# Two-layer trunk kernel: four sums per layer of the down projection's weights stored to DRAM and loaded again

## The reference

```python
for l in range(2):                                   # S = 512 rows, D = 1024, FFN_HIDDEN = 2816
    h = rms_norm(x, pre_mix_g[l]); z = h @ w_in[l]
    y_a = gmlp_mixer(gelu(u), gelu(v), ...)          # spatial gating, 4 groups
    y_b = diff_attention(q, k, v, ...)               # 4 heads, block-causal
    x = x + rms_norm(concat(y_a, y_b) @ w_out[l], post_mix_g[l])
    h = rms_norm(x, pre_ffn_g[l])
    gate, up = split(h @ w_gate_up[l])
    y = (silu(gate) * up) @ w_down[l]                # the stage of this case: 512x2816 times 2816x1024
    x = x + rms_norm(y, post_ffn_g[l])
```

## Time and profile before

| | |
|---|---|
| device time, 3 runs | 1069.54 us median (1069.37 to 1069.75) |
| the profiled execution | 1071.2 us, its span 1069.4 us |
| PE busy | 1058.6 us (99%), granted clock 0.998 |
| PE weight loads busy | 948.2 us |
| DVE, ACT, POOL busy | 789.2, 632.6, 499.0 us |
| DMA | 130.39 MB, mean 122 GB/s |
| raw loads of `w_down` | 54 of 512 KB (4.3 us median to landing), 14 of 256 KB (2.7 us) |
| `x_rows` from `x_spill` | 8 of 512 KB, 5.6 us median |

### The profile page before, as it was taken

One profiled execution on the slowest core, in us unless ns is written; L12 is line 12 of the kernel. 1 busy time (PEld: TensorE's weight loads), 2 busy tenths in 40 slices (PEclk: granted clock), 3 DMA queues, 4 the chain that ended last, 5 costly groups with the idle time before them and its releaser, 6 DMA issues.

```text
span 1069.4 us, 17811 instructions
## 1 busy us (share of the span) xinstructions
PE 1058.6 (99%) x6704; PEld 948.2 (89%) x6704; DVE 789.2 (74%) x1277; ACT 632.6 (59%) x1253; POOL 499.0 (47%) x378
## 2 busy tenths in 40 slices
PE   8999999999999999999999999999999999999997
PEld 7888888999999999888778888889999999998876
DVE  5376644878888886998754756548888888869996
ACT  6767684756555554644657578747555555545352
POOL 4535264457666665030444344634666666630310
PEclk9999999999999999999999999999999999999999
DMA  8423213424334333467353222133343433325662
GB/s 303 141 59 99 70 51 98 158 76 123 92 107 118 90 110 119 150 230 237 123 152 124 79 80 79 60 95 123 100 115 103 118 90 110 118 84 193 219 204 78
DMA packets 151161, 130.39 MB, mean 122 GB/s; under 512 B 4250, under 2 KB 120484, under 8 KB 151076
## 3 DMA queue, kind: packets, MB, share of 16 engines
q1 hardware_dynamic: 151060, 129.25, 38.5%
q10 hardware_dynamic: 16, 0.00, 0.0%
HBM read 122.95 MB, written 6.29 MB: 121 GB/s over the span
## 4 chain that ended last, share of the span: by engine, by line
PE 88%; DVE 7%; DMA 2%; ACT 2%; issue 1%; DVEq 0%; SPq 0%; ACTq 0%
PE banks L720 27%; PE banks L722 27%; PE banks L721 27%; PE banks L789 2%; PE banks L817 2%; DMA raw<-in_w_down_dram 2%; DVE w_lo L2184 2%; PE banks L729 1%; PE banks L802 1%; PE banks L1042 1%; PE banks L828 1%; ACT junk L1263 0%; DVE part_full L2148 0%; DMA x_rows<-in_x_dram 0%; DVE raw L2171 0%
## 5 line engine op out<-in xcount | busy, mean ns | idle before, releaser
L675 POOL TENSOR_TENSOR w_lo<-raw,w_hi 128x512 fp32r<-128x512 f32 x200 | 261.4, 1317 | 146.0 <-ACT w_hi L1338 141.5
L657 POOL TENSOR_TENSOR w_lo<-raw,w_hi 128x512 fp32r<-128x512 f32 x136 | 188.5, 1410 | 294.0 <-ACT w_hi L1255 293.9
L720 PE MATMUL banks<-xg_hi,w_hi 128*128 128x256 f32 (+1 forms) x880 | 273.5, 311 | 0.0
L722 PE MATMUL banks<-xg_lo,w_hi 128*128 128x256 f32 (+1 forms) x880 | 271.3, 308 | 0.0
L721 PE MATMUL banks<-xg_hi,w_lo 128*128 128x256 f32 (+1 forms) x880 | 271.2, 308 | 0.0
L1338 ACT ACTIVATE w_hi<-raw 128x512 fp32r<-128x512 f32 x200 | 124.6, 631 | 116.6 <-DVE raw L2078 62.4
L722 PEld LDWEIGHTS banks<-xg_lo,w_hi 128*128 128x128 f32 x880 | 168.0, 191 | 8.5
L720 PEld LDWEIGHTS banks<-xg_hi,w_hi 128*128 128x128 f32 x880 | 168.1, 191 | 8.3
L721 PEld LDWEIGHTS banks<-xg_hi,w_lo 128*128 128x128 f32 x880 | 168.1, 191 | 7.5
L721 PE MATMUL banks<-s_part,w_lo 128*128 128x256 f32 x480 | 135.8, 283 | 0.0
L720 PE MATMUL banks<-s_part,w_hi 128*128 128x256 f32 x480 | 135.8, 283 | 0.0
(11 more groups left out here) (231 smaller groups left out, 2190.2 us busy)
## 6 DMA issues: line engine op xcount, KB each, us to landing
raw<-in_w_gate_up_dram SPq DMA_DIRECT2D x88, 512.0 KB, 4.2
raw<-in_w_down_dram SPq DMA_DIRECT2D x54, 512.0 KB, 4.3
raw<-in_w_in_dram SPq DMA_DIRECT2D x40, 512.0 KB, 3.8
raw<-in_w_out_dram SPq DMA_DIRECT2D x16, 512.0 KB, 3.4
x_spill<-x_rows SPq DMA_DIRECT2D x8, 512.0 KB, 4.9
x_rows<-x_spill SPq DMA_DIRECT2D x8, 512.0 KB, 5.6
raw<-in_w_down_dram SPq DMA_DIRECT2D x14, 256.0 KB, 2.7
x_rows<-in_x_dram SPq DMA_DIRECT2D x4, 512.0 KB, 7.3
```

Source lines behind the costliest of these rows:

```text
L657: last = tt(lo[:, piece], raw_half(l, c, h)[:, piece], hi[:, piece].bitcast(F32), ALU.subtract)
L675: tt(lo, full, hi.bitcast(F32), ALU.subtract).then_inc(w_ready, 1)
L720: mm(o, stat[0], mov[0], start=first, stop=False)
L722: return mm(o, stat[0], mov[1], start=False, stop=last)
```

## The change

**T2 kept.** For P0 to P3 of each layer, T2 (which `pair_sums` forms anyway) stays in half 1 and is stored to DRAM (`t2_spill`, 256 KB each); T4 is formed in place of B21, by one DVE sum that moves from `pair_sums` into `pair_lows`, ahead of T3's low part. Half 0 of such a P is now loaded again after T4's low part, half 1 after T3's low part and the landed store. Q0 to Q3 load T2 (256 KB) and B22 (256 KB) where B11 (256 KB) and B12 over B22 (512 KB) were loaded, and form T1 = B22 - T2 by one sum.

**x rows.** Row blocks 2 and 3 are reloaded behind the layer's last weight loads, with a semaphore of their own, and so is the next layer's gain `gpre`; `gpost` goes ahead of row block 0.

**Boundary.** After layer 0, ACT's `xg_high(group, 1)` moves ahead of row 2's branch root, and DVE's `xg_low(group, 1)` between the first and second operation of `residual(b, 2)`.

```diff
+    N_KEPT = 4
+        t2_spill = nc.dram_tensor("t2_spill", [L, N_KEPT, P, SE], F32)
...
         def pair_raw(l, c, i):
-            row, col = ((0, 0), (1, 0), (0, 1), (1, 1))[i] if kind == "P" else ((0, 1), (0, 0), (1, 1))[i]
+            row, col = ((0, 0), (1, 0), (0, 1), (1, 0) if t2_kept(c) else (1, 1))[i] if kind == "P" else ((0, 1), (0, 0), (1, 1))[i]
...
         def load_half
-                    if kind_of(d) == "P":
+                    if kind_of(d) == "P" and t2_kept(d):
+                        sp.wait_ge(pair_ready, pair_upto(m, d, P_T3 if h else P_T4))
+                        if h == 1:
+                            sp.wait_ge(t2_stored, 16 * (N_KEPT * m + DOWN[d - C_DOWN][1] + 1))
+                    elif kind_of(d) == "P":
                         sp.wait_ge(pair_ready, pair_upto(m, d, P_T4 if h else P_B21))
...
+            def store_t2(l, c):
+                sp.wait_ge(pair_added, pair_added_upto(l, c, 1))
+                sp.dma_start(t2_spill[l, DOWN[c - C_DOWN][1]], raw_half(l, c, 1)[:, SE:2 * SE]).then_inc(t2_stored, 16)
             def load(l, c):
+                n = raw_n(l, c)
+                if n >= 2:
+                    m, d = RAW_ORDER[n - 2]
+                    if kind_of(d) == "P" and t2_kept(d):
+                        store_t2(m, d)
                 for h in range(2):
                     load_half(l, c, h)
...
-                    for r, behind in enumerate((C_L_END, C_Q[1], C_Q[3], C_Q[5])):
+                    for r, behind in enumerate((C_L_END, C_Q[1])):
...
+                if l < L - 1:
+                    load_gain(gpre[:, :], pre_mix_g[l + 1], gpre_landed)
+                for r in range(2, ST):
+                    sp.dma_start(x_rows[:, r, :], x_spill[r * P:(r + 1) * P, :]).then_inc(x_back_late, 16)
...
         ACT boundary
+                    if r == 2 and b % 2:
+                        xg_high(group, 1)
                     root_of_branch(b, l, r)
-                    if r == 2:
+                    if r == 2 and b % 2 == 0:
                         xg_high(group, 1)
...
         DVE boundary (residual calls between() behind tt(y_b, y_b, silu_t))
-                    residual(b, r)
-                    if r == 2:
+                    if r == 2 and b % 2:
+                        residual(b, r, lambda: xg_low(group, 1))
+                    else:
+                        residual(b, r)
+                    if r == 2 and b % 2 == 0:
                         xg_low(group, 1)
...
         pair_sums
-                        dve.wait_ge(pair_added, pair_added_upto(l, c, 1))
-                        tt(b22, b21, b22, ALU.subtract).then_inc(pair_added, 1)
+                        if not t2_kept(c):
+                            dve.wait_ge(pair_added, pair_added_upto(l, c, 1))
+                            tt(b22, b21, b22, ALU.subtract).then_inc(pair_added, 1)
+                    elif t2_kept(c):
+                        tt(b12, b22, b11, ALU.subtract).then_inc(pair_added, 1)
...
         pair_lows
+                        if kind_of(c) == "P" and t2_kept(c) and i == P_T3:
+                            b21, t2 = [raw_half(l, c, col)[:, SE:2 * SE] for col in range(2)]
+                            dve.wait_ge(pair_added, pair_added_upto(l, c, 1))
+                            tt(b21, b21, t2, ALU.subtract).then_inc(pair_added, 1)
```

More of the change, by code:

```diff
@@ L381, in pair_added_upto, with t2_kept @@
             kind, p = DOWN[c - C_DOWN]
-            return 5 * NP * l + (3 * p + i + 1 if kind == "P" else 3 * NP + 2 * p + i + 1)
+            per_layer = 5 * NP - N_KEPT
+            if kind == "P":
+                return per_layer * l + 3 * p + i + 1
+            return per_layer * l + 3 * NP + 2 * p - min(p, N_KEPT) + i + 1
+        def t2_kept(c):
+            return DOWN[c - C_DOWN][1] < N_KEPT
         def pair_upto(l, c, i):
@@ L531, in weights_of @@
             kind, n = DOWN[c - C_DOWN]
+            if kind == "Q" and n < N_KEPT:
+                if h == 0:
+                    return lambda t: t[:, 0:SE], t2_spill[l, n]
+                return lambda t: t[:, SE:2 * SE], w_dn_v[l, :, 2 * n + 1, HALF:D]
             if kind == "Q" and h == 0:
@@ L553, in load_half @@
                         sp.wait_ge(w_ready, low_upto(m, d, LOW_OF[B22 if h else T4] if blocks(d) else h))
+                if kind_of(c) == "Q" and t2_kept(c) and h == 0:
+                    sp.wait_ge(t2_stored, 16 * (N_KEPT * l + DOWN[c - C_DOWN][1] + 1))
                 view, src = weights_of(l, c, h)
                 sp.dma_start(view(raw_half(l, c, h)), src).then_inc(raw_landed[n % 2][h], 16)
+            def store_t2(l, c):
+                sp.wait_ge(pair_added, pair_added_upto(l, c, 1))
+                sp.dma_start(t2_spill[l, DOWN[c - C_DOWN][1]], raw_half(l, c, 1)[:, SE:2 * SE]).then_inc(t2_stored, 16)
             def load(l, c):
+                n = raw_n(l, c)
[3 more added lines that the diff above has]
+                        store_t2(m, d)
                 for h in range(2):
@@ L1628, in pair_high @@
                     kind, p = DOWN[c - C_DOWN]
-                    if (kind, i) in (("P", P_B11), ("P", P_B21), ("Q", Q_B22)):
+                    loaded = {("P", P_B11): 0, ("P", P_B21): 0, ("Q", Q_B22): 1}
+                    if t2_kept(c):
+                        loaded["Q", Q_T2] = 0
+                    if (kind, i) in loaded:
                         n = raw_n(l, c)
-                        act.wait_ge(raw_landed[n % 2][kind == "Q"], 16 * (n // 2 + 1))
+                        act.wait_ge(raw_landed[n % 2][loaded[kind, i]], 16 * (n // 2 + 1))
+                    elif kind == "P":
+                        act.wait_ge(pair_added, pair_added_upto(l, c, {P_T3: 0, P_T4: 2}[i]))
                     else:
-                        act.wait_ge(pair_added, pair_added_upto(l, c, {P_T3: 0, P_T4: 2}[i] if kind == "P" else i))
+                        act.wait_ge(pair_added, pair_added_upto(l, c, 0 if t2_kept(c) else i))
                     if ring[l, c, i][1] is not None:
@@ L1797, in add_eps, with residual @@
                 ts(bias_a[:, at], ssq_a[:, at], 1.0 / D, EPS, ALU.mult, ALU.add).then_inc(bias_a_ready, 1)
-            def residual(b, r):
+            def residual(b, r, between=lambda: None):
                 y_b = y_right_of(b, r)
@@ L1807, in residual @@
                     tt(y_b, y_b, silu_t[:, r, :], ALU.add).then_inc(y_b_added, 1)
+                    between()
                     if r == 0:
@@ L1819, in residual @@
                 if b % 2 and r == 0:
-                    dve.wait_ge(x_back, 16 * ST * (b // 2 + 1))
+                    dve.wait_ge(x_back, 32 * (b // 2 + 1))
+                elif b % 2 and r == 2:
+                    dve.wait_ge(x_back_late, 32 * (b // 2 + 1))
                 if b % 2:
```

8 lines of the change are left out of this document (4 added, 4 removed).

## The result

| | before | after |
|---|---|---|
| device time, median of 9 runs each | 1069.68 us (1068.67 to 1070.81) | 1071.44 us (1071.09 to 1072.88) |
| the profiled execution, its span | 1071.2, 1069.4 us | 1071.13, 1069.3 us |

The ratio is 1.0020 (1.0011 to 1.0029): 1.8 us slower, where 1067.5 us and a gain of 2 us were forecast.

What follows compares the result with a forecast made beforehand. PE, busy 99% of the span, was taken as the bound, with 3.7 us of stalls to win. Layer 0's 1.1 us and layer 1's 0.95 us made 2.05 us: 1069.5 to 1067.5 us, range 1066.2 to 1070.4 us.

Steps and rivals of the forecast that it cites:

- layer 0's 1.1 us: Layer 0's gain, limited by POOL's lows at the boundary: 1.2 us and not 2.6 us, taken as 1.1 us.
- 0.4 us at Q5 of layer 1: With x row block 3's load moved, Q5's 0.48 us stall in layer 1 goes but for some 0.1 us.
- The left halves: P0 to P3: T4's later sum adds 0.3 us of waits in all, costs PE nothing; thinnest cover 0.8 us.
- signs of being wrong: PE waits before P4 or P5, a store landing after 4 us, Q6's stall unchanged, or no POOL wait at the boundary.
- P0's 0.5 us: P0 ends about 0.5 us later, since T4's sum no longer fills DVE's wait for ACT ahead of `h_low`.
- The third rival: Late release of kept pairs' buffers makes PE wait at P4, P5 and P6: 1073.1 us; chance 0.09.
- P5 loses nothing: Layer 1's P5 had waited 1.56 us for a load and starts near 985.7 again, PE at 989.7.
- The right halves: Q0 to Q3: a 0.69 us sum saved each, counting only at Q0 and Q1; Q2's 0.47 us stall goes.
- The x rows: Moving x loads brings Q6's sums 1.8 us earlier in layer 0; 0.77 us at Q6, 0.6 us at R14 and R18 go.
- put down to the run: The profiled 1071.2 us stood 1.7 us above the median, ascribed to the run; 2.05 us was subtracted from 1069.5 us.
- The boundary: After layer 0, the 0.85 us at row block 1's product goes; POOL's lows then bind with about 1 us wait.
- The first rival: Boundary is free if ACT reaches the second chunk's highs early enough; layer 0 gives 2.5 us: 1065.9 us; chance 0.10.

Runs made afterwards that it cites:

- e3_t2: Kernel before plus only the T2 part, x row blocks and boundary as before: 1071.91 us, +2.2 us, ratio 1.0021 against before.
- e4_no_t2: The whole change without T2 kept (N_KEPT = 0), so moved loads and boundary order only: 1069.92 us, ratio 1.0000 against the kernel before.
- e9_sum_order: Kernel before plus only T4's later sum and the release that follows from it, nothing stored, Q as before: 1075.44 us, ratio 1.0053 against before.
- e10_sum_order_act: e9_sum_order with ACT's two large left-operand highs moved behind P4's and P5's: 1072.48 us, ratio 1.0024 against the kernel before.
- e6_late_release: Kernel before with only half 0 of P0 to P3's raw buffers released at the pair's end: 1069.99 us, ratio 0.9997 against before.
- e14_no_store: The whole change without its eight stores and the waits for them: 1071.71 us, ratio 1.0022 against the kernel before.
- e5_act_order: The whole change with ACT's two large left-operand highs moved behind P4's and P5's: 1070.26 us, ratio 1.0006 against the kernel before.
- e2_boundary: Kernel before plus only the change's order at the boundary: 1070.06 us, ratio 0.9999 against the kernel before.
- e7_early_highs: e4_no_t2 with ACT's two highs of the next layer's second chunk moved around row block 2's root: 1067.70 us, ratio 0.9980 against before.
- e0_before_again: The kernel before, run and profiled once more, unchanged: 1070.11 us, ratio 1.0004.

## Why the prediction was wrong, step by step

Of the 3.9 us between the forecast and the measured time, about 2.7 us lie in T2's part, which was to give some 0.5 us and costs 2.2 us (e3_t2). The rest is most of the gain of 1.5 us forecast for the moved loads and the boundary (layer 0's 1.1 us and 0.4 us at Q5 of layer 1), of which e4_no_t2 shows nothing (1.0000, 0.9992 to 1.0009).

- **The left halves ("this part costs PE nothing").** This is the step that failed and turned the sign. It counted "ACT's 0.63 us for its high part", "under 0.1 us of wait per pair", and looked for danger in the buffers. It never asked what stands behind T4's high on ACT: in P2, two highs of 1.69 us and then P3's. The waits per pair were right (0.09 to 0.10 us). Two of its own signs of being wrong came: PE waits before P5, and a store lands later than 4 us. Gross, the part costs 5.3 us (e9_sum_order), 3.0 us of it ACT's queue (e10_sum_order_act).
- **P0's 0.5 us** were right (0.45 us), and taken as harmless. Together with P4's or P5's data they put DVE's sum behind the start of POOL's lows in layer 0, 1.1 us more; that term was missing (last section).
- **The late release and the store.** The third rival had PE wait at P4, P5 and P6; it waits at P5 of layer 1 alone. "P5 loses nothing" took P3's end as unmoved. P3 ended 1.7 us later (980.87 for 979.15), P5's load went out behind it, and DVE began P5 at 987.17 where "near 985.7 again" was forecast. Alone the late release is free (e6_late_release), and in the change the stores are too (e14_no_store), but the latter because P3 is late. With P3 on time, its store holds back half 1 of P5's load, stores and loads in each other's way as the rival has it, and 0.45 us of the 0.72 us remain (e5_act_order). That the stores cost the change nothing is luck. The Trainium skill's warning (DMA: Bandwidth & Descriptors, section Anatomy of one DMA — SWDGE (gpsimd) path) that a write to HBM can confirm late fits the landing of the change's eight stores after issue,

```profile
DMA to landing us min/median/max: 2.0/2.5/5.0
```

against 2.0 us for the output's. Two took longer than the 4 us I allowed, P3's of both layers (4.8 and 5.0 us). In every run with stores P3's took 4.3 to 5.2 us, and P0's 2.0 us. P3's are issued about 1 us behind the second of P4's two loads, P0's with no weight load in flight; whether the loads or the write itself delays P3's, no run shows. The Trainium skill's fit there, by which 256 KB would take 2.6 us (an estimate), is given for DMAs that GpSimd issues; these are issued by SP.

- **The right halves.** That the sum saved in Q2 is swallowed by ACT's high was right. That little counts of Q0's and Q1's was right for DVE's slack of before and wrong for the delayed DVE: the shorter Qs pay back 3.1 us of the part's own 5.3 us. In layer 1 the sums of Q0 and Q1 gave 1.4 us back as counted, but DVE was 1.7 us late behind P6 (996.11 for 994.38), so it came to Q2 0.3 us later than before (1018.12 for 1017.83) and not 0.9 us earlier. That is why 0.32 us of the stall remain.
- **The x rows.** Mechanism right (0.30 us of wait for 1.49 us), size not: 0.6 us with an interval from 1.8 us to nothing. The 1.7 us by which the profiled execution stood above the median I "put down to the run", and then subtracted stalls of that same run from the median, so that a part of the gain was counted twice. The second profile of the kernel before stood above its median as well, with the same stalls in layer 0. That the runs at the median lack some of them was argued from the profiles of e2_boundary and e6_late_release, and no profile of a median execution of the kernel before shows it.
- **The boundary.** Right: POOL's lows bind, a wait of 1.00 us where about 1 us was named. But alone it is worth nothing (e2_boundary), since it trades one wait for the other. The first rival's condition, ACT's highs early enough, is what e7_early_highs makes true: 2.2 us against e4_no_t2, of which its profiles place 1.2 us at the boundary.

With these the account of the measured time closes, roughly: T2 +2.2 us (e3_t2) and the other parts between -0.6 and +0.2 us, against +1.8 us measured.

## What to carry to other kernels

When an operation moves later by less than a microsecond, list what is queued behind its consumer on every engine, not only what it feeds; a large instruction there carries the delay into the next item. Subtract a stall from a median only if it is in the median's executions: take a second profile, or compare the profiled time with the runs first. Once a part's cost and gain are measured apart (5.3 and 3.1 us here), a small net change shows where to mend; moving two ACT instructions was worth more than any part of the change. A part that a test shows to be free is free in that order only: the stores cost nothing while another delay covers them, and showed once it was mended.

## What the runs showed of the hardware

One DVE sum of 128x1024 takes nearly twice as long when POOL is first. Layer 1 of the profile of before, and of the same kernel in e0_before_again:

```profile
993.80 9.32 POOL L657 TENSOR_TENSOR w_lo<-raw,w_hi 128x512 fp32r<-128x512 f32 x4 [42.49 <-ACT w_hi L1255]
994.38 2.31 DVE L2157 TENSOR_TENSOR hid_full<-hid_hi,part_full 128x1024 f32<-128x1024 f32 x1
```
```profile
992.87 1.22 DVE L2157 TENSOR_TENSOR hid_full<-hid_hi,part_full 128x1024 f32<-128x1024 f32 x1
...
993.69 9.05 POOL L657 TENSOR_TENSOR w_lo<-raw,w_hi 128x512 fp32r<-128x512 f32 x4 [42.46 <-ACT w_hi L1255]
```

In both layers of all 18 traces it takes 1.22 us if it starts ahead of POOL's lows (11 cases) and 2.30 to 2.32 us if behind (25 cases). The sum after it, of the same size and always behind POOL's start, takes 2.2 us in all 36. POOL pays too: four lows take 9.05 to 9.40 us in the rows shown and 5.94 us at the boundary, where DVE has less of this work. The Trainium skill has the rule (SBUF — State Buffer, section Who interferes with whom): a VectorE instruction with two SBUF inputs contends with a GpSimd instruction that reads SBUF, and the one that comes second is blocked. The traces agree, with 1.1 us as the price here. I had not weighed it, since nothing in the diff touches POOL. That this explains a stall that comes and goes (Q2's in the earlier trace rows is in the first of these traces and not in the second) fits, but was argued from the traces; no run delayed DVE here by itself. It is not all of it: in e6_late_release's layer 1 the sum is behind POOL too, and PE loses 0.1 us at Q2.
